# One step of a two-layer hybrid backbone on one core: the first expert pair's rows by a matrix product instead of an indirect fetch, later tables behind the first pair, and the last four adaLN units spread

## The reference

```python
sh_a, sc_a, g_a, sh_f, sc_f, g_f = _ada(c, w_ada[i], b_ada[i])
out = attention(modulate(x, sh_a, sc_a))        # layer 0;  fourier_mix(...) in layer 1
x = layernorm(ALPHA * x + g_a * out) * gain + bias
t = modulate(x, sh_f, sc_f)
# top-1 of 4 groups by t @ w_rg, top-2 of 8 experts in it by t @ w_re -> combine (n, 32)
act = silu(t @ w_g[e]) * (t @ w_u[e]) * combine[:, e]
x = layernorm(ALPHA * x + g_f * sum_e(act @ w_d[e])) * gain + bias
```

## Time and profile before

| what | value |
|---|---|
| median of 3 runs | 1004.77 us (1003.29 to 1006.99) |
| the profiled execution's own time | 1004.65 us |
| its span, first to last instruction | 1002.8 us |
| PE busy | 840.4 us (84%) |
| DVE, POOL, ACT busy | 342.4, 164.2, 140.4 us |
| weight queue (q1) | 287.84 MB, 72.8% of 16 DMA engines |
| read and written in DRAM | 313.62 MB and 32.05 MB |

### The profile page before, as it was taken

How to read it: one execution, slowest core, us unless ns; L and a number is a source line. 1 busy time by engine, 2 the same in 40 slices (tenths; PEclk the granted TensorE clock), 3 DMA queues, 4 the chain that set the end, 5 groups by cost and what they waited for, 6 DMA issues and landing times.

```text
span 1002.8 us, 12751 instructions
## 1 busy us (share of the span) xinstructions
PE 840.4 (84%) x4891; PEld 431.5 (43%) x4891; DVE 342.4 (34%) x832; ACT 140.4 (14%) x327; POOL 164.2 (16%) x250
## 2 busy tenths in 40 slices
PE   3899999999897898988787888999599878786954
PEld 3556666655467333333333335646433423232321
DVE  2113454556586111110101049377511111111136
ACT  0122222223010101110101021001111100110110
POOL 1041212123111120111111101121201111111000
PEclk9989999999997999998989899998599989999977
DMA  9997493448259997999999959885799999999941
GB/s 335 366 356 271 130 381 125 142 182 322 97 196 383 381 406 286 416 419 419 419 418 418 381 223 388 330 335 198 295 379 418 418 420 418 419 419 419 384 170 63
DMA packets 91756, 324.54 MB, mean 324 GB/s; under 512 B 12654, under 2 KB 25678, under 8 KB 67608
## 3 DMA queue, kind: packets, MB, share of 16 engines
q1 hardware_dynamic: 73936, 287.84, 72.8%
q0 software_dynamic: 12704, 21.86, 6.1%
q10 hardware_dynamic: 5032, 13.71, 3.5%
HBM read 313.62 MB, written 32.05 MB: 345 GB/s over the span
## 4 chain that ended last, share of the span: by engine, by line
PE 53%; DMA 30%; DVE 9%; issue 3%; ACT 2%; SPq 1%; POOL 1%; ACTq 0%; POOLq 0%; DVEq 0%
PE psum L1010 17%; DMA ring<-in_w_expert_up 16%; PE psum L890 8%; PE psum L837 6%; PE psum L1032 5%; DMA h_hT<-in_w_expert_up 5%; DMA ring<-in_w_ada 4%; PE psum L786 4%; PE psum L862 3%; DMA arena<-h_scratch,gidx 2%; PE psum L994 2%; PE psum L1103 1%; PE psum L941 1%; DMA h_hT<-y_scratch 1%; PE psum L919 1%
## 5 line engine op out<-in xcount | busy, mean ns | idle before, releaser
L1010 PE MATMUL psum<-ring,arena 128*64 128x512 f32 x880 | 266.1, 650 | 36.9 <-DMA ring<-in_w_expert_up 27.7
L1010 PEld LDWEIGHTS psum<-ring,arena 128*64 128x64 f32 x880 | 89.0, 149 | 172.5 <-issue 167.1
L1032 PE MATMUL psum<-ring,arena 128*64 128x512 f32 x440 | 124.1, 598 | 20.1 <-DVE arena L1788 19.5
L1784 DVE TENSOR_TENSOR arena<-arena,psum 128x256 f32<-128x256 f32 x34 | 14.3, 421 | 294.4 <-ACT arena L1342 294.4
L1010 PE MATMUL psum<-h_hT,arena 128*64 128x512 f32 x208 | 98.1, 627 | 10.1 <-DMA ring<-in_w_expert_up 9.3
L890 PE MATMUL psum<-ring,h_hT 128*128 128x384 f32 x288 | 98.1, 494 | 0.0
L837 PE MATMUL psum<-ring,h_hT 128*128 128x512 f32 x160 | 70.7, 603 | 3.7 <-DVE h_hT L1952 2.2
L890 PEld LDWEIGHTS psum<-ring,h_hT 128*128 128x128 f32 x288 | 54.4, 194 | 35.0 <-issue 1.6
L650 POOL DMA_INDIRECT y_scratch<-arena,sidx x32 | 32.6, 1019 | 217.4 <-DVE arena L1794 217.4
L1032 PEld LDWEIGHTS psum<-ring,arena 128*64 128x64 f32 x440 | 35.6, 136 | 71.3 <-issue 46.9
L786 PE MATMUL psum<-ring,silu 128*32 128x128 f32 x1536 | 53.7, 301 | 15.0 <-DMA ring<-in_w_ada 15.0
(11 more groups left out here) (215 smaller groups left out, 885.5 us busy)
## 6 DMA issues: line engine op xcount, KB each, us to landing
ring<-in_w_expert_down SPq DMA_DIRECT2D x52, 1024.0 KB, 25.7
ring<-in_w_expert_gate SPq DMA_DIRECT2D x50, 1024.0 KB, 17.9
ring<-in_w_expert_up SPq DMA_DIRECT2D x50, 1024.0 KB, 24.0
ring<-in_w_ada SPq DMA_DIRECT2D x24, 2048.0 KB, 14.9
h_hT<-in_w_expert_gate SPq DMA_DIRECT2D x12, 1024.0 KB, 18.2
h_hT<-in_w_expert_up SPq DMA_DIRECT2D x12, 1024.0 KB, 24.1
h_hT<-in_w_expert_down SPq DMA_DIRECT2D x12, 1024.0 KB, 26.7
ring<-in_w_qkv SPq DMA_DIRECT2D x9, 1024.0 KB, 12.3
```

Of the source, the lines that this page charges most:

```text
L1010: last = pe.matmul(bank[b][64 * e:64 * e + 64, :].rearrange("p (g n) -> p g n", g=2), mem.GT[b][:, c, 64 * e:64 * e + 64], w, start=(c == ...
L1032: last = pe.matmul(bank[5 + half][64 * e:64 * e + 64, :], mem.actT[b][:, f, 64 * e:64 * e + 64], w[:, f, 512 * half:512 * half + 512], sta ...
```

## The change

1. **First pair.** DVE makes, right after the position product, a 0/1 matrix `pick[0]` (tokens by the 128 rows of pair 0; two instructions). PE multiplies `mem.h` by it, 24 products of 128 x 128, straight into the two PSUM banks that `gt` would fill. The fetch of pair 0 and its transposes go; the fetches that are left count one lower. The table of the first passes is computed after that product.
2. **Later tables.** The table of the further passes, the transposes of the selection matrix and `columns(1)` on PE move behind pair 0's `gate_up`; DVE's selection matrix moves behind the counts and words, `rest_of_table` behind pair 0's product `up_times`. POOL waits for that last table (`table_done` 3) before it releases the output buffers and enters its loop. `passes` runs pair 0 before it reads the words that say how many further passes there are.
3. **SP.** Expert 2 of layer 0 waits for pair 1's rows alone; expert 4 for pair 0's product.
4. **adaLN.** Of layer 1's last four units only 9 stays ahead of the cosine products; 8 goes behind them, 10 and 11 behind the last router product. Unit 8 is loaded before 10. Experts 0 and 1 of layer 1 are now issued first (projection done), experts 2 and 3 after unit 11.
5. **Gates and end.** Layer 1's second gates are spread after its tables. In layer 1 `scale_rows` and the three `keep` come behind pair 15's SiLU, product and eviction, no longer in between.

The waits that only renumber, and PSUM bank changes, are left out here.

```diff
 def passes(eng, l, S, first, body):
+    first(0, 0)
     word = words(eng, l)
     for n in range(PAIRS):
-        if n < LAST:
+        if 0 < n < LAST:
             first(n, n % 2)
...
-def first_rows_fetched(l):
-    for b in range(2):
-        sp.wait_ge(main[l][f"gathered{b}"], 16)
 def load_last_slot(l):
-    first_rows_fetched(l)
+    sp.wait_ge(main[l]["gt_ps"], 1)
     sp.wait_ge(logits_ps, 2 * l + 2)
...
 after_ada(1, 5)
-first_rows_fetched(0)
+sp.wait_ge(main[0]["gathered1"], 16)
 for e in (2, 3):
...
 after_ada(1, 6)
+load("ada", 1, 8)
+sp.wait_ge(sums_read, TILES)
 load("ada", 1, 10)
-sp.wait_ge(sums_read, TILES)
-load("ada", 1, 8)
 after_ada(1, 7)
 load("ada", 1, 11)
+sp.wait_ge(proj_ps, 12)
+for e in (0, 1):
+    load_expert(1, e)
 after_ada(1, 11)
 for e in (2, 3):
-    load_expert(1, e)
-sp.wait_ge(proj_ps, 12)
-for e in (0, 1):
     load_expert(1, e)
...
         if l == 1:
             pool.wait_ge(four_ps, 4)
             router_weights(1)
+if l == 0:
+    pool.wait_ge(proj_used, 6)
+    for i in range(2):
+        spread(mem.gates[:, i, :], 0, 5, i, gates_in[i])
+pool.wait_ge(scratch_out, ZEROED + 16 * TILES * (l + 1))
+pool.wait_ge(table_done, 3 * l + 1)
+gather(S, l, 1, 0, 1)
+if l == 0:
+    store_m(1, 4, 6, ADA_AT[1, 5], landed=False)
+pool.wait_ge(table_done, 3 * l + 3)
+pool.sem_inc(S["o_free"], 2)
 if l == 1:
     store_m(1, 10, ADA_UNITS, ADA_AT[1, 11])
-pool.wait_ge(proj_used, 6 * (l + 1))
-for i in range(2):
-    spread(mem.gates[:, i, :], l, 5, i, gates_in[i])
-pool.wait_ge(scratch_out, ZEROED + 16 * TILES * (l + 1))
-pool.wait_ge(table_done, 3 * l + 1)
-for m in range(2):
-    gather(S, l, m, m, m)
-if l == 0:
-    store_m(1, 4, 6, ADA_AT[1, 5], landed=False)
-pool.wait_ge(table_done, 3 * l + 2)
-pool.sem_inc(S["o_free"], 2)
+    pool.wait_ge(proj_used, 12)
+    for i in range(2):
+        spread(mem.gates[:, i, :], 1, 5, i, gates_in[i])
...
 gate_up(S, n, n, b, gate_up_landed(n), second_half_landed(n))
+if n == 0:
+    pe.wait_ge(ada_done, ADA_AT[1, (5, 11)[l]])
+    if l == 0:
+        columns(1)
+    table(l, 1)
 if n < LAST:
-    gt(S, n + 1, 16 * ((n + 1) // 2 + 1), 1 - b)
-elif l == 1:
-    kept(0)
+    gt(S, n + 1, 16 * ((n + 2) // 2), 1 - b)
+if n == 0:
+    pe.wait_ge(table_done, 3 * l + 2)
+    if l == 0:
+        pe.wait_ge(col_done, 3)
+    for t in range(TILES):
+        last = pe.transpose(bank[7][:, P * t:P * t + P],
+                            mem.pick[0][:, t, :, :].rearrange("p e s -> p (e s)"), ident)
+    last.then_inc(table_ps, 1)
 act_transposes(S, n, b)
...
 router(l, 2).then_inc(logits_ps, 1)
+for u in ((2, 3, 4), (10, 11))[l]:
+    ada(1, u)
 if l == 0:
-    for u in (2, 3, 4):
-        ada(1, u)
     pe.wait_ge(tables_in, 16)
...
-                dst = out[CAP * e:CAP * e + CAP, 0:n]
-                last = pe.matmul(dst if rest == 0 else dst.rearrange("p (r n) -> p r n", n=PAIRS),
-                                 mem.row_hot[:, c, :], at, start=(c == 0), stop=(c == 2 * TILES - 1))
-        last.then_inc(table_ps, 1)
     if l == 0:
         ada(1, 5)
-    pe.wait_ge(table_done, 3 * l + 3)
-    for t in range(TILES):
-        last = pe.transpose(bank[6][:, P * t:P * t + P], mem.pick[0][:, t, :, :].rearrange("p e s -> p (e s)"), ident)
+    pe.wait_ge(placed_done, 3 * l + 1)
+    for c in range(KC):
+        for t in range(TILES):
+            last = pe.matmul(bank[2 + c // 4][:, P * (c % 4):P * (c % 4) + P], mem.h[:, t, c::KC],
+                             mem.pick[0][:, t, :, :].rearrange("p e s -> p (e s)"),
+                             start=(t == 0), stop=(t == TILES - 1))
+    last.then_inc(main[l]["gt_ps"], 1)
+    table(l, 0)
+def table(l, rest):
+    pe.wait_ge(placed_done, 3 * l + 2 + rest)
+    out, n = ((bank[6], PAIRS), (bank[1], (PASSES - 1) * PAIRS))[rest]
+    for c in range(2 * TILES):
+        for e in range(2):
+            at = mem.placed[:, c, 0, e::2] if rest == 0 else mem.placed[:, c, 1:, e::2]
+            dst = out[CAP * e:CAP * e + CAP, 0:n]
+            last = pe.matmul(dst if rest == 0 else dst.rearrange("p (r n) -> p r n", n=PAIRS),
+                             mem.row_hot[:, c, :], at, start=(c == 0), stop=(c == 2 * TILES - 1))
...
 over_positions(1)
-for u in (9, 8, 10, 11):
-    ada(1, u)
-pe.wait_ge(ada_done, 2 * ADA_UNITS)
+ada(1, 9)
 for half in range(2):
     pe.wait_ge(chan_act, 4 + half + 1)
     pe.wait_ge(chan_dve, half + 1)
+    if half == 1:
+        pe.wait_ge(ada_done, ADA_AT[1, 9])
     cosines(1, half, True)
     four = slice(4 * half, 4 * half + 4)
     out = bank[SINE_BANKS[half]].rearrange("p (g n) -> p g n", g=4)
     pe.matmul(out[:, :, 0:1], chan[:, 1, 0, :], mem.U[:, 1, four, P:P + 1], start=True, stop=True)
     pe.matmul(out[:, :, 1:], chan[:, 1, 1, :], mem.U[:, 1, four, P + 1:], start=True, stop=True
               ).then_inc(four_ps, 1)
+ada(1, 8)
 pe.wait_ge(four_sb, 4)
 mixer_to_experts(1)
...
 pos = bank[1][:, 0:TILES * EXPERTS].rearrange("p (t e) -> p t e", t=TILES)
+place = mem.first_w.rearrange("p (t e) -> p t e", t=TILES)
+link(V.scalar_tensor_tensor(out=place, in0=pos[:, :, 0:2], scalar=1.0, in1=mem.Msum[:, :, 0:2],
+                            op0=ALU.add, op1=ALU.mult))
+shape = [P, 2 * TILES, CAP]
+V.scalar_tensor_tensor(out=mem.pick[0].rearrange("p t e s -> p (t e) s"),
+                       in0=bc(mem.const("row64").unsqueeze(1), shape), scalar=1.0,
+                       in1=bc(mem.first_w.unsqueeze(2), shape), op0=ALU.add, op1=ALU.is_equal
+                       ).then_inc(placed_done, 1)
...
 last.then_inc(placed_done, 1)
+gt_evict(main[l], 0, 0)
+dve.wait_ge(table_ps, 3 * l + 1)
+V.tensor_scalar(mem.table[:, 0:PAIRS], bank[6][:, 0:PAIRS], float(INVALID), None, ALU.add
+                ).then_inc(table_done, 1)
 for k in range(2):
     for t in range(TILES):
         c, shape = TILES * k + t, [P, PASSES - 1, EXPERTS]
         last = V.tensor_tensor(mem.placed[:, c, 1:, :], bc(mem.M[k][:, t, :].unsqueeze(1), shape),
                                bc(mem.pass_id[:, c, 1:].unsqueeze(2), shape), ALU.mult)
 last.then_inc(placed_done, 1)
-def table_evict(part, src):
-    V.tensor_scalar(mem.table[:, part], src, float(INVALID), None, ALU.add).then_inc(table_done, 1)
-dve.wait_ge(table_ps, 3 * l + 1)
-table_evict(slice(0, PAIRS), bank[0][:, 0:PAIRS])
 dve.wait_ge(count_ps, l + 1)
...
-    dve.wait_ge(table_ps, 3 * l + 2)
-    table_evict(slice(PAIRS, PASSES * PAIRS), bank[1][:, 0:(PASSES - 1) * PAIRS])
     link(V.tensor_reduce(mem.words_f[:, :], mem.further.rearrange("p (h n) -> p h n", h=2), AX, ALU.add))
     V.tensor_copy(mem.words[:, :], mem.words_f[:, :]).then_inc(words_done, 1)
+    for u in (range(2, 6), range(10, ADA_UNITS))[l]:
+        ada_add(1, u)
+def rest_of_table(l):
+    dve.wait_ge(table_ps, 3 * l + 2)
+    V.tensor_scalar(mem.table[:, PAIRS:PASSES * PAIRS], bank[1][:, 0:(PASSES - 1) * PAIRS], float(INVALID), None,
+                    ALU.add).then_inc(table_done, 1)
+def selection(l):
     link(V.scalar_tensor_tensor(out=mem.first_w, in0=mem.r6[:, 1], scalar=0.0,
...
-if n == LAST and l == 1:
-    keep(l, 0)
-    keep(l, 1)
 up_times(S, n, b)
+if n == 0:
+    if l == 0:
+        columns(1)
+    rest_of_table(l)
 if n < LAST:
     gt_evict(S, n + 1, 1 - b)
 at_evict(S, n, b)
 if n < LAST:
     o_evict(S, n, b)
 else:
-    keep(l, 0 if l == 0 else 2)
+    for t in range((1, TILES)[l]):
+        keep(l, t)
     gated_evict(S, l)
```

More of the change, by code:

```diff
@@ L1088, in picked @@
                                   mem.gated[i][:, 512 * half:512 * half + 512], start=alone, stop=True).then_inc(sums_ps, 1)
-                gt(S, 0, 16, 0)
+                passes(pe, l, S, first, body)
+                kept(0)
                 pe.wait_ge(route_out, 3 * l + 3)
-                passes(pe, l, S, first, body)
-                if l == 0:
-                    kept(0)
                 picked(0)
@@ L1149, in mixer_to_experts @@
                 last.then_inc(count_ps, 1)
-                for rest, out, n in ((0, bank[0], PAIRS), (1, bank[1], (PASSES - 1) * PAIRS)):
-                    pe.wait_ge(placed_done, 2 * l + 1 + rest)
-                    for c in range(2 * TILES):
-                        for e in range(2):
-                            at = mem.placed[:, c, 0, e::2] if rest == 0 else mem.placed[:, c, 1:, e::2]
-                            dst = out[CAP * e:CAP * e + CAP, 0:n]
-                            last = pe.matmul(dst if rest == 0 else dst.rearrange("p (r n) -> p r n", n=PAIRS),
-                                             mem.row_hot[:, c, :], at, start=(c == 0), stop=(c == 2 * TILES - 1))
-                    last.then_inc(table_ps, 1)
                 if l == 0:
                     ada(1, 5)
-                pe.wait_ge(table_done, 3 * l + 3)
-                for t in range(TILES):
-                    last = pe.transpose(bank[6][:, P * t:P * t + P], mem.pick[0][:, t, :, :].rearrange("p e s -> p (e s)"), ident)
+                pe.wait_ge(placed_done, 3 * l + 1)
```

(20 more changed lines are left out.)

14 lines of the change are left out of this document (7 added, 7 removed).

## The result

The changed kernel took 1012.11 us (median of 4 runs, 1009.57 to 1012.69) against 1004.92 for the kernel before on the same chip: 1.0069 times as long, 95% interval 1.0051 to 1.0087. The forecast was 1001.0, with a range up to 1008.5; the prediction is wrong, in sign and in size.

A forecast was written before the change was run, and what follows sets the result against it. Bound by the expert stages' weight streams (DMA full at 418 GB/s), by PE and DVE elsewhere. From 1004.65 us, layer 0 +2.9, layer 1's stream -5.6 and the end -0.9 gave 1001.0, range 993.5 to 1008.5.

The forecast's parts named there:

- Layer 0, the step that failed: Layer 0's expert stage: a late further pass of pair 0 delays the weight loads; 2.9 us lost.
- The new product: Layer 0's first pair: 48 PE records, about 2 us cold and the rest warm, 7.1 us in all.
- Unit 5 ahead of it: Layer 0, adaLN unit on PE before the new product: about 2.5 us from 312.6, to 315.1.
- The larger effect is pair 0's further pass: Layer 0: its table behind gate/up sends its fetch at 334.4 instead of 327.6; its gate/up starts 2.9 us later.
- its own signs: Moments and durations named in advance for the profile after, mostly in layer 0, to show whether the prediction held.
- the product cold throughout: Layer 0, part of the bound of 10 us lost: the new product all at the low clock, +4.4 us.
- rival C: Layer 1's stream gains nothing, late loads and POOL's queue eat the lead; 1005.5 us or so, chance 0.16.
- Rival B: Layer 0: the further pass becomes the bound, product cold, fetch takes 12.1 us; +10, 1008.2 us, chance 0.12.
- Layer 1's mixer: Layer 1's mixer and routing: fewer adaLN units ahead of the cosine products bring projection and routing 11.0 us earlier.
- Layer 1's stream: Layer 1's expert weights: expert 4 can follow at 722.3 and no gap opens; 5.6 us gained.
- the end: End of layer 1: pair 15's product and eviction no longer between the `keep` steps; 0.9 us gained.
- rival D: Layer 1: PE's lead of 14 us reaches the end, the stream not being the bound; 992.7 us, chance 0.06.

The follow-up runs named there:

- e4_old0: The changed kernel with layer 0's entry as before the change, layer 1 and the end as after it: 1000.05 us, ratio 0.9958 to the kernel before.
- e1_contig: The changed kernel with the new product reading 128 neighbouring columns as stationary operand (feature order left out): 1005.75 us, ratio 1.0002.
- h1_step2: The changed kernel with the product's stationary operand read with a step of 2 elements instead of 8 (feature order left out): 1005.9 us, one execution.
- e3_fetch2: The changed kernel with pair 2's fetch of layer 1 issued right behind pair 1's: 1011.08 us, ratio 1.0062.
- e2_ada5: The changed kernel with unit 5 of adaLN moved behind the product and first table of layer 0: 1006.38 us, ratio 1.0012.
- f2_front: The changed kernel with contiguous product operand (ACT copies), unit 5 behind layer 0's first table, and the rest of that table ahead of pair 0's gate/up: 994.50 us.
- f4_old01: The changed kernel without the product: both layers fetch both pairs' rows as before, adaLN units spread as after the change: 1001.43 us, ratio 0.9949.
- g1: f2_front with pair 2's fetch of layer 1 issued right behind pair 1's: 994.87 us, ratio 0.9908.
- g2: f2_front with adaLN unit 11 ahead of layer 1's projection and expert 2 of layer 1 loaded beside it: 994.37 us, ratio 0.9910.
- f3: e4_old0 with adaLN unit 11 ahead of layer 1's projection and expert 2 of layer 1 loaded beside it: 1004.60 us, ratio 0.9999.

## Why the prediction was wrong

**Layer 0, the step that failed.** Forecast +2.9, bounds -2.4 to +10; e4_old0 puts it at +11 to +12. Three terms of it failed, and the experiments price them:
- The new product, 7.1 us with bounds 6 and 10.8: it took 11.73, outside both. The warm row that I scaled has the same form on the page, but its stationary operand is contiguous. The diff shows the stepped slice; the prediction put its cost at nothing. Repaired, it is 6.4 us of the total in the two layers. With the contiguous form the same 48 records took 5.60 to 7.25 us: the forecast fits that kernel. So does a page's price (the Trainium skill, "FP8 and Floating Point Precision", TensorE Precision Notes, by which I estimated 5.1 us): the trace comes near it at 5.60 with a contiguous operand and is more than twice as long with the stepped one. The stepped slice was in the diff, and I had not weighed it.
- Unit 5 ahead of it, "2.5 us, to 315.1": I took its weights as landed. The DMA issues of the kernel before, asked for this load alone (count, KB, us to landing), say otherwise:

```profile
ring<-in_w_ada SPq DMA_DIRECT2D x1, 2048.0 KB, 27.4
```

It was issued at 289.3, so it landed at 316.7, 4.1 us behind the 312.6 at which I had the unit start; the 19.2 us that I had read was the median of two loads, of 11.0 and 27.4. Before, both tables and a wait stood ahead of the unit until 318.03 and hid it. With the unit ahead of it the product started 8.5 to 13.4 us behind the position product (e1_contig and h1_step2 at the one end, e3_fetch2 at the other; the forecast has 4.7), and 2.5 us behind it in e2_ada5. Putting the product behind the unit cost 5.7 us, the wait and the unit's own time together.
- "The larger effect is pair 0's further pass", at 7 us later for its fetch: right as a mechanism. It cost 3 to 4 us as the change stands and 7.8 behind a short product. Beside the late rows, the pass ran cold behind PE's idle time of 5 us (granted clock 0.50 from 348.2 to 356 us), which I had no term for: its transposes took 1.97 us instead of the 1.16 in f2_front, and its gate/up 9.83 instead of the 7.09 of the earlier trace rows.

By its own signs the prediction failed here too: the 48 records took 11.73 us (6.5 to 8.5 were named), experts 2 and 3 went out at 334.71 (327.5 to 329), the further pass's gate/up started at 351.18 (345 to 349) and SP's issue behind it at 403.89 (395 to 398). Three sums in it are slightly off and decide nothing: the product cold throughout is 3.7 us more and not 4.4, by its own ends of 7.1 and 10.8; rival C, 5 us worse than the sum, is 1006.0; and 5.1 us for the product are 2.0 less than 7.1.

**Rival B** (the further pass bound, the product cold, +10, 1008.2) was nearest in place and size, but its cause was another: not the clock but the weight load. It stopped short because I took 1.2 GHz as the slowest that a product can be.

**Layer 1's mixer**: cosines forecast for 642.3 plus layer 0's loss, projection 27.5 us, a lead of 11.0. Measured 651.71 with layer 0 9.2 us late (so 642.5 without), 27.73 and 10.9: right. f4_old01 shows that the product has no part in it: from the first adaLN load behind layer 0 to expert 0's issue are 79.3 us there, 79.7 in the changed kernel and 90.5 before.

**Layer 1's stream**: -5.6, bounds 2 to 8 gained, and the end -0.9; together -6.5. e4_old0 measured -4.2 by the ratio and -5.4 by the medians (1000.05 against 1005.40 beside it). The gap of rival C came where it said, behind POOL's queue, but it is worth 1 to 2 us (e3_fetch2), not 5. That the lead of PE can't be cashed (against rival D) is right: f4_old01 starts pair 0 5 us later, relative to expert 0's issue, at no measurable price. From the load of the last rows to the end of the span took 40.4 us against 41.0; no experiment took this edit alone, so that it comes from the moved `keep` is argued, not shown.

**The chances**: I gave B 0.12. A new operation without a row of its own, on the path, ahead of everything else in the stage, deserved a wider upper bound.

## What to carry to other kernels

Before a moved instruction is priced, ask what the instruction now ahead of it waits for: a late load that nobody waited for costs time once something is queued behind it, 5.7 us here. When a new product is scaled from an old row, compare the layout of both operands: a step of 16 or 32 bytes in the stationary one, or of 32 in the moving one, doubled this one. And where a stream of weights is bound by bytes and by a late fetch at once, either repair alone can show nothing: g1 and g2 would each have been dropped (f3, on a slower kernel, even lost 4 us), and together they gave 4 us.
